# A hybrid decoder layer on one core: the low part of the down weights made one step later, and the last block's first loads paced in groups of three

## What is computed

```python
# routing gives 8 of 64 experts to each token; the pairs (token, expert) are sorted by expert
# and padded per expert to whole blocks of 128 rows
def body(acc, blk):
    toks, bw, e = blk
    xb = hp[toks]
    yb = (jax.nn.silu(xb @ w_gate[e]) * (xb @ w_up[e])) @ w_down[e]
    return acc.at[toks].add(yb.astype(f32) * bw[:, None]), None
...
shared = (jax.nn.silu(hf @ ws_gate) * (hf @ ws_up)) @ ws_down
h = _layernorm(ALPHA * h + (acc + shared), ln2_g, ln2_b)
```

## Time and profile before

| | |
|---|---|
| median of 3 runs | 2506.89 us (2502.52 to 2510.63) |
| the profiled execution, its own time | 2510.86 us |
| its span, first to last instruction | 2509.0 us |
| mean granted TensorE clock | 0.973 of full speed |
| steps of the expert loop, 889 to 2390 us | 162 |
| last block | from about 2395 us on |

### The profile page before, as it was taken

How to read it: one execution, slowest core, us unless ns; L and a number is a source line. 1 busy time by engine, 2 the same in 40 slices (tenths; PEclk the granted TensorE clock), 3 DMA queues, 4 the chain that set the end, 5 groups by cost and what they waited for, 6 DMA issues and landing times. The chain is left out here.

```text
span 2509.0 us, 49346 instructions
## 1 busy us (share of the span) xinstructions
PE 2357.9 (94%) x11266; PEld 1904.2 (76%) x11268; DVE 1758.6 (70%) x2382; ACT 1179.1 (47%) x1863; POOL 972.2 (39%) x772
## 2 busy tenths in 40 slices
PE   8899999999998799999999999999999999999966
PEld 6576777678886677888778887787778888877855
DVE  6686767758878767667767677667766677767437
ACT  3525253532225545455554545545554546545334
POOL 0010100011110155554555555554655556555437
PEclk9999999979998899999999999999999999999988
DMA  6143434465655478878887878888888789887796
GB/s 252 76 168 122 137 116 141 136 222 196 216 206 208 167 240 269 248 220 271 254 269 232 260 232 247 272 261 257 255 241 249 226 240 300 274 247 229 180 248 202
DMA packets 165327, 551.13 MB, mean 220 GB/s; under 512 B 31344, under 2 KB 56080, under 8 KB 144784
## 3 DMA queue, kind: packets, MB, share of 16 engines
q1 hardware_dynamic: 109696, 355.03, 40.1%
q0 software_dynamic: 54960, 195.27, 31.0%
q10 hardware_dynamic: 608, 0.02, 0.0%
HBM read 394.99 MB, written 155.25 MB: 219 GB/s over the span
## 5 line engine op out<-in xcount | busy, mean ns | idle before, releaser
L2647 PE MATMUL psG<-gu_split,xT_hi 128*128 x2624 | 626.0, 391 | 3.4 <-ACT xT_hi L2421 1.9
L2647 PEld LDWEIGHTS psG<-gu_split,xT_hi 128*128 128x128 f32 x2624 | 494.9, 189 | 107.5 <-issue 4.1
L1669 POOL DMA_INDIRECT xg<-hcut,gi x332 | 376.6, 1134 | 144.0 <-issue 92.5
L2661 PE MATMUL psG<-gu_split,xT_lo 128*128 x1304 | 341.2, 403 | 0.0
L2526 DVE TENSOR_TENSOR gu_split<-raw_gu,gu_split (+1 forms) x127 | 289.4, 2279 | 69.2 <-ACT gu_split L2444 59.5
L2406 POOL DMA_INDIRECT acc<-y,si x81 | 170.4, 2104 | 413.1 <-DVE y L2602 376.5
L2661 PEld LDWEIGHTS psG<-gu_split,xT_lo 128*128 128x128 f32 x1304 | 233.1, 189 | 42.4
L2444 ACT ACTIVATE gu_split<-raw_gu x126 | 234.4, 1908 | 33.2 <-issue 16.6
L2510 DVE STREAM_TRANSPOSE xF<-xg 128x1024 f32<-128x1024 f32 x82 | 177.2, 2161 | 91.8 <-DMA xg<-hcut,gi 91.7
L2526 DVE TENSOR_TENSOR d_lo<-raw_d,d_hi (+1 forms) x64 | 146.6, 2291 | 123.9 <-ACT d_hi L2444 123.9
L2699 PE MATMUL psY<-d_hi,HT_lo 128*128 x648 | 204.3, 397 | 18.8 <-DVE HT_lo L2589 18.8
(11 more groups left out here) (404 smaller groups left out, 4038.9 us busy)
## 6 DMA issues: line engine op xcount, KB each, us to landing
raw_gu<-in_w_gate_dram SPq DMA_DIRECT2D x64, 1024.0 KB, 5.2
raw_gu<-in_w_up_dram SPq DMA_DIRECT2D x64, 1024.0 KB
raw_d<-in_w_down_dram SPq DMA_DIRECT2D x64, 1024.0 KB
wring<-split_d SPq DMA_DIRECT2D x24, 1024.0 KB, 5.8
second<-blank SPq DMA_DIRECT2D x17, 512.0 KB, 6.8
split_d<-wring POOLq DMA_DIRECT2D x8, 1024.0 KB, 4.2
raw_d<-mixed SPq DMA_DIRECT2D x16, 512.0 KB, 5.3
xt<-in_x_dram SPq DMA_DIRECT2D x16, 512.0 KB, 5.7
```

The costliest lines, as they stand in the source:

```text
L1669: nc.gpsimd.indirect_dma_start(out=to[:, g, 0:PIECE], out_offset=None, in_=hcut.rearrange("r a w -> (r a) w"), in_offset=bass.IndirectOffs ...
L2647: nc.tensor.matmul(psG[slot][:], xT_hi[slot][:, c, :], right[:, bass.ds(w, 1), c, :].rearrange("p a n -> p (a n)"), start=(n == 0 and c == ...
L2661: m = nc.tensor.matmul(psG[slot][:], xT_lo[slot][:, c, :], gu_hi[:, bass.ds(w, 1), c, :].rearrange("p a n -> p (a n)"), start=False, stop= ...
```

## The change

On DVE, piece 2 (the low part of the down weights, `split(..., 2)`) goes from the end of step n, where it was made for the word of block n+1, to the middle of step n, for the word of block n: one step later, behind the product and `turn_x`, and ahead of piece 0 and of the copy of y. The words are read from the turn's first block on, so indexes grow by one. In the last block, SP's loads of group g, from g = 2 on, wait until the late tile of group g-2 has had its second table added.

```diff
@@ preamble of DVE
             when_first(dve, block0, lambda: split(block0, 1))
-            when_first(dve, block0, lambda: split(block0, 2))
             when_first(dve, block1, lambda: split(block1, 0))
@@ body of DVE
-                nexts = entries(dve, i * TURN + 1, TURN + 1)
+                words = entries(dve, i * TURN, TURN + 2)
...
                     if k == 0:
-                        pair_weight(nexts[n + 1], s.turn + 2, 0)
-                        pair_weight(nexts[n], s.turn + 1, 1)
+                        pair_weight(words[n + 2], s.turn + 2, 0)
+                        pair_weight(words[n + 1], s.turn + 1, 1)
                     product(s.n + 2, 1 - k, s.turn + 1 + k)
                     if k == 0:
                         turn_x(s.turn + 2)
-                    when_first(dve, nexts[n + 1], lambda: split(nexts[n + 1], 0))
+                    when_first(dve, words[n], lambda: split(words[n], 2))
+                    when_first(dve, words[n + 2], lambda: split(words[n + 2], 0))
                     s.wait(dve, yps_s[1])
                     dve.wait_ge(added[k], s.turn * 16)
                     nc.vector.tensor_copy(y[k][:, 512:], psY[:, 1, :]).then_inc(y_s[1], 1)
-                    when_first(dve, nexts[n + 1], lambda: split(nexts[n + 1], 1))
-                    when_first(dve, nexts[n], lambda: split(nexts[n], 2))
+                    when_first(dve, words[n + 2], lambda: split(words[n + 2], 1))
@@ last block, SP
             for g in range(LATE):
+                if 2 <= g:
+                    sp.wait_ge(z_all[EARLY + g - 2], 16)
                 for t in (2 * g, 2 * g + 1):
                     if t < EARLY:
                         load_z(t)
```

## The result

The changed kernel takes 2656.73 us (median of 4 runs, 2651.84 to 2659.22) against 2506.25 us for the kernel before beside it: a ratio of 1.0597, interval 1.0574 to 1.0621. Slower was forecast, but 2560 us, and the range ended at 2582. The loss is 150 us and not 53.

What follows compares the result with a forecast made beforehand. PE, busy 1464.0 of 1501 us, bounds the expert loop; in 21 slow turns a ring through DVE, POOL and DMA sets the pace. 45.6 + 8 + 0 + 0 - 1 = +52.6 us on 2506.9 gave 2560, range 2524 to 2582.

Steps and rivals of the forecast that it cites:

- The ring: Slackless loop through DVE, POOL and DMA (y copy, scatter, gathers, landing, turn_x, piece 0, y copy), 19.78 us a round.
- turns A: 21 two-step turns, even block n and n+2 both first of their expert: piece 2 adds 2.17 us each, 45.6 us.
- the rival in which the ring gives: Gathers land in 4.4 us, not 5.9, once the down load moves away; 15 us, 2525 to 2530; 12 in 100.
- B: 15 turns where only even block n is first: 13 overrun their slack before the down products; 8 us, bounds 0 and 15.
- The last block: After the loop, the waits put on SP's loads: -1 us, bounds -3 and +6.
- The rival on the other side: The removed d_hi wait was what held DVE up, so PE regains 18.8 + 11.6 us: 2477 us; 8 in 100.
- turns C: 26 turns where odd block n+1 is first: piece 2 fits in DVE's idle time or the copy's room; put at 0.
- both upper bounds: Upper bounds of the even steps with a lone first block (15 us) and of the odd steps (13 us).
- the single even steps: 15 even steps with a first block at n alone: 1.61 us spare against 2.17; 0.6 us in each of 13, 8 us.
- odd steps: 26 odd steps where piece 2 runs beside the gathers: 0 taken, 13 us (16 x 0.8) as upper bound.
- D: 15 turns where only even block n+2 is first: put at 0.
- Weights come late: Moved down load pushes gate and up loads, up to 4.2 us in each of 21 turns: 88 us, 2648; 5 in 100.

Runs made afterwards that it cites:

- a1: DVE's new order alone, without the paced loads of the last block, against the kernel before: 2646.67 us, ratio 1.0572.
- a2: The kernel before with only the paced loads of the last block added, DVE's order as before: 2506.90 us, ratio 1.0012.
- a3: Piece 2 moved only where the first block is even, no paced loads, against the kernel before: 2635.63 us, ratio 1.0552.
- c1: The kernel before, piece 2 unmoved; three reductions (1.8 us) ahead of y's copy in even steps with an expert's first block: 2631.9 us, ratio 1.0512.
- a4: Piece 2 moved only where the first block is odd, no paced loads, against the kernel before: 2538.05 us, ratio 1.0131.
- d1: The kernel before with the loop's gate, up and down loads all cut to 64 KB (output wrong): 2459.63 us.
- b2: a1 with the copy of y ahead of pieces 2 and 0, timed against the kernel before: 2578.29 us, ratio 1.0253.
- b4: Piece 2 one step later but at the step's end behind piece 1, last block as before, against the kernel before: 2604.29 us, ratio 1.0369.
- e2: a1 with only gate and up loads cut to 64 KB (output wrong): 2543.06 us, 55.3 above the order before with the same cut.
- e4: a1 with only down loads cut to 64 KB (output wrong): 2653.33 us, 148.1 above the order before with the same cut.
- d2: a1 with gate, up and down loads all cut to 64 KB (output wrong): 2492.20 us, 32.6 above d1.
- p1: The kernel before with POOL issuing both gathers of every turn ahead of both scatters: 2705.84 us, ratio 1.0811.

## Why the prediction was wrong

**What held.** The ring of the earlier trace rows in the turns A, and both priced terms. A: forecast 45.6, measured 45.3 (51.7 in a1, so the tenths are luck). A turn A goes from 20.0 to 22.2 us on average (17.86 + 45.0/21 and 17.86 + 90.3/21), and its gathers land 6.0 us after the last issue in both kernels, so the rival in which the ring gives is out. B: forecast 8, measured 7.3 in these turns' own length. The last block: forecast -1 with -3 and +6 as bounds; it is 0.6 us longer, its first mean is made 49.7 us after the last start of the down products, before 49.1, and a2 shows no gain. DVE's wait for d_hi is gone and bought nothing. The rival on the other side (2477) is out with it: it needed gathers that land within 3.7 us of their last issue, and in the turns A of the changed kernel they took 5.8 to 6.5 us.

**What did not show in the profile after as forecast, even in A.** DVE's wait for the gather was to go up by 2 to 4 us in each of the 21 turns. It fell, from 2.3 to 0.7 us on average; the rise of the sum, 91.7 to 188.1 us, is from the turns C. And the range's upper end does not follow from its reason: with both upper bounds half taken the sum stands near 2570, and 2582 needs both whole and the ring at 2.29 us (7 + 13 + 2.5).

**The step that failed** is how far a late copy and a late gather were followed: in each case only to the end of their own step. It has two places.

The larger is the single even steps' "I take 0.6". The 0.6 us is right for the step itself (B, 7.3 us in sum), but the same paragraph has no term for what the late copy does to POOL: the scatter and the four gathers of the odd step behind it. That was put at nothing without a reason. It is the turns C that pay: +66 us in a3, where nothing of theirs was moved, and +83 in c1, where nothing was moved at all.

The smaller is the one on odd steps: "a late gather, up to 1.4 us later, can delay the `turn_x` of the next even step. I take 0 ... and keep 13 us (16 x 0.8) as upper bound". No row gives the 0.8. In a4 the odd steps alone cost 34 us: C is 20 us longer and D 14.

Both price the lateness of an issue at the same lateness of the landing, or less. The measured landing is not a shift of the issue. Among whole loads it also goes from at most 4.1 us to over 6 (the table above), `turn_x` then waits some 6 us, and the next copy, scatter and gathers are late in their turn.

The profile before held two warnings. One is the 5.9 us of the landing in the ring, against at most 4.4 in the undisturbed turn: I looked at the down load as its cause (the first rival) and not at the gate and up loads ahead of the gathers. The other is the longest wait of DVE for the gather, the 5.7 us in the earlier trace rows, which I did not look up. It stands in a turn C, step 98, whose length is 4.1 us over 17.86, and it shows the whole case:

```profile
1801.54 0.33 SPq L2359 DMA_DIRECT2D raw_gu<-in_w_gate_dram  x1
...
1802.11 0.33 SPq L2359 DMA_DIRECT2D raw_gu<-in_w_up_dram  x1
...
1802.26 0.95 POOL L1669 DMA_INDIRECT xg<-hcut,gi  x1 [0.30 <-issue]
...
1809.52 2.13 DVE L2510 STREAM_TRANSPOSE xF<-xg 128x1024 f32<-128x1024 f32 x1 [5.68 <-DMA xg<-hcut,gi]
```

**The chances.** "Weights come late" had 5 in 100 and 2648 us, near the time that was measured, but for another reason: ACT does not wait for weights (1.7 us in 4 waits for raw_gu, before 16.6 in 31). It is the gathers that land late. "If the 15 single even steps lose several microseconds each" was named among what would make the prediction wrong; it was the turns behind them that lost, 3.3 us for each of the 26 of C.

**What the wait does to PE** was no term of the sum. PE is idle for 96.1 us more and is busy for 60.9 us longer with the same work, at a granted clock of 0.97 where it had 1.00. Idle time of PE in this loop costs about 1.6 times its length (157.0 / 96.1). The clock is most of the 60.9, by an estimate: a mean of 0.97 between the two levels means some 6% of 1648 us, about 100 us, at the lower one, where a matmul takes up to twice as long (1.2 against 2.4 GHz), so up to 50 us. For the same reason the forecast's 37 us for what could be given back was low: in d1 PE is never idle (0.1 us) and the loop is 45.8 us shorter than before, since its busy time falls too, from 1455.6 to 1444.7.

**Which is shown and which is argued.** Shown: even first blocks carry most of it (a3, a4); a late y without any moved piece brings C (c1), and taking piece 2 from ahead of the copy takes most of C away (b2, b4); C needs the gate and up loads (e2 against e4); with small loads only A is left (d2: +38, before it in d1 +4). Not shown: where in the DMA the gathers lose the time, in a queue behind the megabytes or in a slower read of the table. The gathers' slowdown beside DVE (0.95 us to 2.4 to 3.0) is part of how they come to be late, but no run took it away alone. In A two paths cost about the same (the ring, and HT_lo in b2 and b4), and no run separates them in the changed kernel itself.

## What to carry to other kernels

When a change makes a small transfer later, don't price it by the delay: look up which large transfers are issued just behind it, and price the landing with these close by and with their order turned round. Here that was a wait of 3 and of 6 us for a copy 2 us late, and it repeated itself, because the late landing made the next issue late again. Look up the longest wait of a row, too, and not only its mean: here one of 39 already was the case to come. And a turn whose slack is read as enough (here 1.6 us, with 2.17 to pay) should be followed through the next turn's waits before it is priced at the difference.

## What the runs showed of the hardware that was not expected

Four gathers landed 2.1 to 2.4 us after the end of their last issue in 20 turns of e2, with gate and up loads of 64 KB issued 2.1 us behind the start of that issue, and 4.4 to 4.9 us after it in 3 turns with the same order and loads of a megabyte. They landed 6.2 to 8.3 us after it in the 23 turns of the kernel before and of the changed one in which two loads of a megabyte had been issued just ahead of the last one. In p1 a scatter whose issue overlapped those of the two loads was landed only 10 us after its own issue had ended (1175.94 to 1185.93).

POOL's issue of a gather takes 0.95 us alone (the median). What slows it is starting while a DVE subtraction of pieces runs, both of whose operands lie in SBUF: the 29 such gathers of the kernel before took 1.90 to 3.05 us. The gather at 1019.00 started in the subtraction that ran from 1018.72 to 1021.01 and ended at 1021.84; the one at 1022.14 started in that from 1021.53 to 1023.81 and ended at 1024.63. Each ended 0.8 us after the subtraction. A gather that was already running when the subtraction began was not slowed: 60 of them in the kernel before took 0.94 to 0.99 us, among them the one at 1571.83 with d_lo at 1571.95. The Trainium skill (SBUF — State Buffer, "Who interferes with whom") infers that such a subtraction leaves descriptor writing alone, and says in the same section that it contends with a GpSimd instruction that reads SBUF. These gathers read their indices (gi) there. The slow issue is against the inference if it is the writing that waits, and in line with the other sentence if it is the reading; no run here tells the two apart.

After PE's wait for the copy of y in front of 1035.63 (2.38 us) its granted clock was 0.66 over the 5 us from 1036 and 1.00 behind them; over the loop the same matmuls kept PE busy 4.2% longer (1455.6 to 1516.6 us).
